# One-core diffusion backbone: the mask of local attention added in PSUM, softmax weights scaled on VectorE, and a reciprocal root taken as a power on GpSimd

## The reference

```python
def window_attention(q, k, v, kc, vc, sink):      # 8 heads of 64; one key head for 4 query heads
    valid = (abs(kj - T - qi) <= WINDOW) & (kpos >= 0) & (kpos < L)      # WINDOW = T = 128
    s_loc = where(valid, einsum(q, k) * scale, NEG)                      # scale = 1/8
    s_ctx = einsum(q, kc) * scale
    p = softmax(concatenate([s_loc, s_ctx, s_sink], -1))
    return einsum(p_loc, v) + einsum(p_ctx, vc)

def retention_out(o, g):                          # 8 heads of 64
    o = o * rsqrt(mean(o * o, -1) + EPS)
    return o * silu(g)
```

## Time and profile before

| | |
|---|---|
| median of 3 runs | 2737.83 us (2731.96 to 2738.38) |
| the profiled execution's own time | 2735.59 us |
| its span, first to last instruction | 2733.9 us |
| PE / DVE / ACT / POOL busy | 92% / 44% / 32% / 4% |
| mean granted TensorE clock | 0.950 of full speed |
| from the first score to the first product of the output projection | 914.36 to 1098.70 us |

### The profile page before, as it was taken

The page is one execution under the profiler, slowest core; times in us unless marked ns, Lnnn a source line. Parts: engine busy times, 40 slices in busy tenths (PEclk is TensorE's granted clock), DMA queues, the critical chain, the costliest instruction groups (busy, mean ns, idle before and its releaser), DMA issues.

```text
span 2733.9 us, 32899 instructions
## 1 busy us (share of the span) xinstructions
PE 2504.0 (92%) x12514; PEld 1971.3 (72%) x12514; DVE 1209.1 (44%) x1765; ACT 876.5 (32%) x1283; POOL 111.7 (4%) x186
## 2 busy tenths in 40 slices
PE   5899999999899887899999989999989828899997
PEld 2477788899778434778877778778878527788886
DVE  4523233565553676543222353323355385533334
ACT  1422222444431456343222242222244302422222
POOL 1011000000000110000011000100000000000000
PEclk9999999999999899889999989999979969799999
DMA  7566322455312000132356312552212113132322
GB/s 289 196 219 226 128 96 75 151 176 183 130 62 83 31 1 1 62 108 85 100 200 224 130 58 93 193 181 94 91 55 93 70 46 107 49 102 81 108 77 77
DMA packets 91167, 309.53 MB, mean 113 GB/s; under 512 B 10960, under 2 KB 11632, under 8 KB 89776
## 3 DMA queue, kind: packets, MB, share of 16 engines
q1 hardware_dynamic: 67824, 221.75, 24.2%
q0 software_dynamic: 21936, 84.88, 8.7%
q10 hardware_dynamic: 1296, 1.38, 0.1%
HBM read 299.58 MB, written 8.39 MB: 113 GB/s over the span
## 4 chain that ended last, share of the span: by engine, by line
PE 81%; DVE 8%; ACT 4%; DMA 2%; issue 2%; POOLq 0%; POOL 0%; DVEq 0%; ACTq 0%
PE psum L451 24%; PE psum L452 23%; PE psum L453 23%; PE psum L582 2%; DMA mod_raw<-in_w_mod 2%; PE psum L460 2%; PE psum L873 1%; DVE spectrum L359 1%; DVE term L352 1%; PE psum L740 1%; PE psum L604 1%; DVE w_lo L1297 1%; PE psum L862 1%; DVE stats L1767 1%; ACT w_hi L893 0%
## 5 line engine op out<-in xcount | busy, mean ns | idle before, releaser
L451 PE MATMUL psum<-h_hi,w_hi 128*128 128x512 f32 (+1 forms) x2256 | 860.4, 381 | 28.4 <-DVE h_lo L1480 13.7
L452 PE MATMUL psum<-h_lo,w_hi 128*128 128x512 f32 (+1 forms) x2256 | 848.4, 376 | 0.0
L453 PE MATMUL psum<-h_hi,w_lo 128*128 128x512 f32 (+1 forms) x2256 | 847.5, 376 | 0.0
L451 PEld LDWEIGHTS psum<-h_hi,w_hi 128*128 128x128 f32 x2256 | 429.3, 190 | 128.1 <-issue 35.1
L1297 DVE TENSOR_TENSOR w_lo<-raw,w_hi 128x1024 fp32r<-128x1024 f32 (+2 forms) x442 | 470.6, 1100 | 65.3 <-ACT w_hi L893 61.4
L893 ACT ACTIVATE w_hi<-raw 128x1024 fp32r<-128x1024 f32 (+2 forms) x442 | 405.8, 951 | 251.2 <-PE psum L453 243.7
L453 PEld LDWEIGHTS psum<-h_hi,w_lo 128*128 128x128 f32 x2256 | 429.1, 190 | 77.2
L452 PEld LDWEIGHTS psum<-h_lo,w_hi 128*128 128x128 f32 x2256 | 429.8, 191 | 74.0 <-issue 1.0
L451 PE MATMUL psum<-act_hi,w_hi 128*128 128x512 f32 (+1 forms) x880 | 331.5, 377 | 7.5 <-DVE w_lo L1297 5.5
L453 PE MATMUL psum<-act_hi,w_lo 128*128 128x512 f32 (+1 forms) x880 | 329.2, 374 | 0.0
L452 PE MATMUL psum<-act_lo,w_hi 128*128 128x512 f32 (+1 forms) x880 | 329.1, 374 | 0.0
(11 more groups left out here) (229 smaller groups left out, 1812.5 us busy)
## 6 DMA issues: line engine op xcount, KB each, us to landing
raw<-in_gate_up SPq DMA_DIRECT2D x220, 512.0 KB, 4.2
mod_raw<-in_w_mod POOLq DMA_DIRECT2D x144, 512.0 KB, 5.6
raw<-in_down_a SPq DMA_DIRECT2D x80, 384.0 KB, 3.5
raw<-in_down_b SPq DMA_DIRECT2D x80, 320.0 KB, 3.0
raw<-in_hy_in SPq DMA_DIRECT2D x24, 512.0 KB, 3.5
raw<-in_mix_in SPq DMA_DIRECT2D x22, 512.0 KB, 3.5
filt_dram<-made SPq DMA_DIRECT2D x6, 1024.0 KB, 3.8
filt<-filt_dram POOLq DMA_DIRECT2D x2, 3072.0 KB, 10.9
```

The source lines that it names most:

```text
L451: pe.matmul(out, w_hi[:, slot, c:c + P], hi, start=start, stop=False)
L452: pe.matmul(out, w_hi[:, slot, c:c + P], lo, start=False, stop=False)
L453: return pe.matmul(out, w_lo[:, slot, c:c + P], hi, start=False, stop=stop)
```

## The change

1. **Mask in PSUM.** `score` adds the mask to the own-key scores by one or two more matmuls (identity x mask tile, 128 columns each) in the same accumulation. The own keys now end where the context keys begin, so that the whole row is one stretch of PSUM (`score_row`). The masked score is scaled afterwards.
2. **Softmax order.** `take` is now only a maximum over PSUM and a small operation for the exponent's bias; `exps` reads PSUM and scales there. The division by the row sum moves from ACT to DVE, behind `take` of the next unit; ACT's order becomes `copy_out(s-1)`, `exps(s)`.
3. **Reciprocal root.** `root` on ACT becomes a scale and add (Identity); the four DVE reciprocals go; GpSimd raises the 128x512 tile to the power -0.5 in one instruction for each pair of heads.

```diff
-                    pe.matmul(psum[:, a, 0:(hi - lo) * P], q, k[:, lo * P:hi * P], start=True, stop=True)
+                    own = psum[:, a, SEQ - (hi - lo) * P:SEQ]
+                    pe.matmul(own, q, k[:, lo * P:hi * P], start=True, stop=False)
+                    if lo < n:
+                        pe.matmul(own[:, 0:P], ident[:, :], mask[:, 0:P], start=False, stop=hi == n + 1)
+                    if hi > n + 1:
+                        pe.matmul(own[:, (hi - lo - 1) * P:(hi - lo) * P], ident[:, :], mask[:, 2 * P:3 * P], start=False, stop=True)
...
                     act.wait_ge(scores_read, u + 1)
-                    act.activation(probs[:, i, 0:w], probs[:, i, 0:w], ACT.Exp, bias=stats[:, i, 1:2],
+                    if u >= 2:
+                        act.wait_ge(probs_turned, u - 1)
+                    act.activation(probs[:, i, 0:w], score_row(u), ACT.Exp, bias=stats[:, i, 1:2], scale=QK_SCALE,
                                    accum_out=stats[:, i, 2:3])
...
-                def normalize(u):
-                    w, i = window(u)[4], u % 2
-                    act.wait_ge(rsum_ready, u + 1)
-                    act.activation(probs[:, i, 0:w], probs[:, i, 0:w], ACT.Copy, scale=stats[:, i, 5:6]).then_inc(probs_ready, 1)
...
-                    act.activation(full[:, 1, :], psum[:, 7, :], ACT.Sqrt, bias=eps[:, 0:1],
+                    act.activation(full[:, 1, :], psum[:, 7, :], ACT.Identity, bias=eps[:, 0:1],
...
                     if 1 <= s <= UNITS:
-                        normalize(s - 1)
+                        copy_out(s - 1)
                     if s < UNITS:
                         exps(s)
-                    if 1 <= s <= UNITS:
-                        copy_out(s - 1)
...
-                    dve.scalar_tensor_tensor(probs[:, i, 0:own], psum[:, 2 * i, 0:own], QK_SCALE, mask[:, m:m + own], ALU.mult, ALU.add)
-                    seq(dve.tensor_scalar(probs[:, i, own:w], psum[:, 2 * i + 1, 0:CTX], QK_SCALE, None, ALU.mult))
-                    seq(dve.tensor_reduce(stats[:, i, 0:1], probs[:, i, 0:w], AX.X, ALU.max))
+                    seq(dve.tensor_reduce(stats[:, i, 0:1], score_row(u), AX.X, ALU.max))
...
-                    dve.reciprocal(stats[:, i, 5:6], stats[:, i, 4:5]).then_inc(rsum_ready, 1)
+                    seq(dve.reciprocal(stats[:, i, 5:6], stats[:, i, 4:5]))
+                    dve.tensor_scalar(probs[:, i, 0:w], probs[:, i, 0:w], stats[:, i, 5:6], None, ALU.mult).then_inc(probs_ready, 1)
...
-                    dve.reciprocal(full[:, 0, part], full[:, 1, part]).then_inc(dve_step, 1)
...
+            pool.memset(power[:, :], -0.5).then_inc(power_set, 1)
...
+            def invert(t):
+
+                pool.wait_ge(orms_ready, t + 1)
+                pool.tensor_tensor(full[:, 0, :], full[:, 1, :], power[:, 0:1].to_broadcast([P, SEQ]),
+                                   ALU.pow).then_inc(inv_ready, 1)
```

More of the change, by code:

```diff
@@ L208, in build @@
         stats = sb("stats", [P, 2, 8])
+        neg_sink = sb("neg_sink", [P, HEADS])
+        power = sb("power", [P, 1])
         filt_dram = nc.dram_tensor("filt_dram", (2, P, 3, 4, 512), F32).ap()
@@ L330, in build, with score_row @@
         osq_ready, osum_ready, orms_ready, oval_ready = map(sem, ("osq_ready", "osum_ready", "orms_ready", "oval_ready"))
+        def score_row(u):
+            i, w = u % 2, window(u)[4]
+            both = psum[:, 2 * i:2 * i + 2, :].rearrange("p b c -> p (b c)")
+            return both[:, SEQ + CTX - w:SEQ + CTX]
         def products(eng, step_sem, step, c, i, part, t0, t1, done, before):
@@ L731, in attention_retention @@
                 pe.wait_ge(result_read, at["p"] + BANKS)
+                pe.wait_ge(side_loaded, 32)
                 def score(u):
@@ L1759, in take @@
                 def take(u):
-                    h, n, lo, hi, w = window(u)
-                    own, m, i = w - CTX, (lo - n + 1) * P, u % 2
+                    h, i = window(u)[0], u % 2
                     dve.wait_ge(scores_ready, u + 1)
-                    if u >= 2:
-                        dve.wait_ge(probs_turned, u - 1)
-                    dve.scalar_tensor_tensor(probs[:, i, 0:own], psum[:, 2 * i, 0:own], QK_SCALE, mask[:, m:m + own], ALU.mult, ALU.add)
-                    seq(dve.tensor_scalar(probs[:, i, own:w], psum[:, 2 * i + 1, 0:CTX], QK_SCALE, None, ALU.mult))
-                    seq(dve.tensor_reduce(stats[:, i, 0:1], probs[:, i, 0:w], AX.X, ALU.max))
-                    dve.tensor_scalar(stats[:, i, 1:2], stats[:, i, 0:1], sink[:, h:h + 1], -1.0, ALU.max,
-                                      ALU.mult).then_inc(scores_read, 1)
+                    seq(dve.tensor_reduce(stats[:, i, 0:1], score_row(u), AX.X, ALU.max))
+                    dve.tensor_scalar(stats[:, i, 1:2], stats[:, i, 0:1], -QK_SCALE, neg_sink[:, h:h + 1], ALU.mult,
+                                      ALU.min).then_inc(scores_read, 1)
                 def normalize(u):
@@ L1805, in weigh @@
                         corner_of(2 * t + 3)
-                def invert(t, part):
-                    dve.wait_ge(orms_ready, t + 1)
-                    part = slice(part * P, part * P + P)
-                    dve.reciprocal(full[:, 0, part], full[:, 1, part]).then_inc(dve_step, 1)
-                    at["step"] += 1
                 def finish(t):
-                    dve.wait_ge(dve_step, at["step"])
+                    dve.wait_ge(inv_ready, t + 1)
                     seq(dve.tensor_tensor(prod[:, 0, :], prod[:, 0, :], full[:, 0, :], ALU.mult))
@@ L1825, in attention_retention @@
                 dve.wait_ge(gate_ready, 2)
+                seq(dve.tensor_scalar(neg_sink[:, :], sink[:, :], -1.0, None, ALU.mult))
                 corner_of(0)
@@ L1830, in attention_retention @@
                         att_out((s - 10) // 8)
+                    if s < UNITS:
+                        take(s)
                     if 1 <= s <= UNITS:
                         normalize(s - 1)
-                    if s < UNITS:
-                        take(s)
                     if s - INVERTED - 3 in PAIR_END:
@@ L1839, in attention_retention @@
                             weigh(i)
-                    for part in range(4):
-                        if s - 2 - part in PAIR_END:
-                            invert(PAIR_END.index(s - 2 - part), part)
                     if s - 2 - INVERTED in PAIR_END:
@@ L1960, in _ @@
                     ins.then_inc(table_ready, 1)
+                if t:
+                    invert(t - 1)
+            invert(HEADS // 2 - 1)
             pool.wait_ge(x_ready, 24)
```

3 lines of the change are left out of this document (2 added, 1 removed).

## The result

The changed kernel takes **2986.42 us** (median of 4 runs, 2984.69 to 2990.32) against 2735.37 (2731.96 to 2738.38) for the kernel before beside it: ratio 1.092, 95% interval 1.0901 to 1.094. It is 251 us slower. The prediction had the direction right, but at 2791 (2744 to 2862) not the size.

What follows compares the result with a forecast made beforehand. The prediction took the mixer's stage to be bound by a chain between engines. Order +4, power's hold +42 and half clock +8 gave +54 on 2735.6, 2789.6; with 2.2 for the median, 2791 us, range 2744 to 2862.

Steps and rivals of the forecast that it cites:

- the price of the power: GpSimd's power for each pair: 15 us long, 4.6 of it free, so 4 x (15 - 4.6) = +42.
- the rival with "30 us or more": GpSimd's power far longer, 30 us or more: over +116, 2855 and up; chance 0.10.
- The mechanism: A running GpSimd power holds VectorE's sum and scaling, now on the chain before the transposes, until it ends: +42.
- a power that doesn't hold VectorE: Rival: the power is hidden, within the free 4.6 us or not holding VectorE: +4, 2742; chance 0.20.
- a remark: By its dependencies the power holds up little: `finish` comes 22 us after `root`, the last wanted some 16 us after.
- The half clock term (8): TensorE at half clock behind four holes of 10 us left by the powers, about 2 each: +8.
- The order of the softmax: Mask products and the new softmax order in the mixer's stage, without the power: +4, bounds -4 to +12.
- The clear steps: Score-to-score times without stalls: long units 5.6 even, 6.4 to 6.6 odd; short 4.8 and 5.7 to 5.8.
- The decay adds on the chain: GpSimd's decay adds meet VectorE's sum and scaling on the chain, once for each of three pairs: +4.5.
- The old stalls of 24: Stalls before the change from decay tables, function table switches, held VectorE adds and half clock: 24 us, taken as gone.
- +1.5 for half clock at the start: TensorE's mask products at half clock at the start of the stage: +1.5.
- The rival "TensorE's rest is not in series": Mixer steps return to 5.16 and 4.46 without stalls, power hidden: about 2715; chance 0.05 for faster by over 0.3%.

Runs made afterwards that it cites:

- the multiply kernel: The changed kernel with GpSimd's power replaced by a plain multiply of the same tile, so the root is left out: 2745.39 us, ratio 1.0052.
- the kernel with short adds: The changed kernel with a multiply for the power, and GpSimd's decay adds of the last three pairs on 32 of 512 columns: 2739.25 us, ratio 1.002.

## Why the prediction was wrong, and where it was right

**The step that failed is the price of the power.** "A power is a logarithm and an exponential at least, so I take 15 us, with 7 and 30 as the ends": it is 81.93 us, 5.5 times the estimate and 2.7 times its upper end. The estimate scaled VectorE's reciprocal (5.9 times a plain operation) to GpSimd; against GpSimd's plain add of 1.26 the power is 65 times as long. No row of before was near it, the upper end of 30 had nothing behind it, and the rival with "30 us or more" had a chance of 0.10.

**The mechanism failed too.** "A power of 15 us would hold it for what is left of 15 us": it holds nothing. The prediction had named this sign itself (sums that stay at 0.16 beside a running power), and what came was a mixture of two of its rivals: a power that doesn't hold VectorE, and one far longer than 30 us. The row behind it was read rightly (a VectorE add held to the end of a GpSimd add; short and long plain adds both bear it out), but it was carried over from one operation to another. The Trainium skill ("SBUF — State Buffer", section "Who interferes with whom") gives the ports that VectorE and GpSimd share to one instruction as a lock for its whole length, and names VectorE's instructions with two SBUF inputs, as the sum is, among those that need them. These runs agree for plain adds (sum 1.02, scaling 1.27) and disagree for the power (0.15 and 0.55 beside it), and the measurement decides. Why the power doesn't hold them wasn't tried.

**What did set the price** stands in the prediction as a remark: `finish` comes 22 us after `root`, and the last one is wanted 16 us after. With a power of 81.9 us these slacks give 3 x 60 + 66 = 246, and 2735.6 + 4 + 246 + 2.2 = 2988, 1.4 above the measured median. That it comes so near is luck in part: the order was +14 and not +4, and the waits 242 and not 246. Measured waits are 57.1, 57.9, 58.4 and 68.9, slacks 24.8, 24.1, 23.5 and 13.0. The hold would have made the power's price 4 x (81.9 - 4.6) = 309. So with the right size and the wait of `finish` in place of the hold, the sum would have come out within a few us. The half clock term (8) isn't to be seen in the difference: the kernel with power is 241.0 above the one with a multiply, its waits 241.5. Half clock does stand behind the holes (the transposes at 1056.97, behind 58.71 idle, take 1.33), but in the multiply kernel they take 1.33 at that place too, behind the hole that the decay adds leave, and the step that follows takes 7.01 in both.

**The order of the softmax** was +4 (-4 to +12) and measured +14 without the root's cost (+18 with it), just outside its bounds. The clear steps were right: 5.34 to 5.51 and 6.39 to 6.61 for long ones (5.6; 6.4 to 6.6), 4.8 to 5.0 and 5.64 for short ones (4.8; 5.7 to 5.8); eight of them from step 3 on make 44.7 in the kernel with short adds (44.4). Mis-sized are its stalls. The decay adds on the chain were put at 4.5 and gave 6.1. "The old stalls of 24 are not in it" was only partly so: from the third to the last score the multiply kernel takes 173.9 where 161 and the 4.5 were expected, and 168.6 remain with short adds. Two single steps make some 3 us of the rest: the third score's own takes 6.99, its products at half clock, where other even long steps take 5.34 to 5.51 (the prediction's +1.5 for half clock at the start belongs there), and step 29 takes 8.01 where other odd long steps take 6.39 to 6.61 (9.68 in the kernel with short adds). What remains is spread and wasn't taken apart. Steps 28 and 29 have no retention scores. TensorE's rows there, in the multiply kernel:

```profile
1084.99 0.76 PE L761 MATMUL psum<-ident,probs 128*128 128x128 f32 x5 [2.02 <-DVE probs L1781]
...
1090.36 0.77 PE L761 MATMUL psum<-ident,probs 128*128 128x128 f32 x5 [2.02 <-DVE probs L1781]
1091.05 1.86 PE L774 MATMUL psum<-probs_t,av 128*64 128x128 f32 x20
1092.69 1.06 PE L795 MATMUL psum<-sumsq,rv 128*64 128x512 f32 x1
```

With nothing to do between score and transposes, TensorE is idle for 2.02 twice, and then `pv` takes 1.86 instead of 1.31, at a mean granted clock of 0.61 from 1091 to 1094; the sum had no term for such a step. The tail (+1.2) was right, from the last score to the projection 10.45 against 9.27; the gain of 1.4 at the start didn't come (the first two steps 12.1 against 11.9). Two slips in the prediction's sums change nothing: 2789.6 + 2.2 is 2791.8, and "4 x 25 + 12" is 112 and not over 116.

**Where the order's own parts go.** The prediction took its cost as one chain, and the runs split it: mask in PSUM -12.6, VectorE's scaling 0, copy ahead of exps -5, `take` ahead of `normalize` +32, the root's loads and reciprocals gone -4. They add up to +10 where +14 was measured, as near as runs of three sets can be added; the -4 is small too, since the runs of its two kernels overlap (2741.95 to 2747.64 and 2745.44 to 2754.05). One exchange of two calls on VectorE eats the gains of all others and more. The rival "TensorE's rest is not in series" set its mark at "when the transposes start by T + 2.5". With them at T + 2.78 an even step is 4.49, so the mark was about right, but its mechanism wasn't: in that kernel TensorE's products follow one another in series without an idle time, and the step is short because nothing in the series waits for VectorE. The change was one exchange of two calls away from it.

## What to carry to other kernels

When an operation is moved to an engine on which no row shows it, price it by its slack instead of by a guess at its length: say how long it may be before somebody waits (here 13 to 25 us), and give no upper end to what it may cost beyond that; a run with a single short instruction of that kind on that engine would have settled it. In an in-order queue, put the work whose consumer is idle now (sum and scaling of the last row) ahead of the work for the next round; here that is worth 32 to 36 us out of 2730, more than the mask (12.6) or the root's reciprocals (4) gained. A contention seen between two operations is a fact about these two and is to be measured again for a third.

## What the runs showed of the hardware

- GpSimd's power of f32 takes 20.74, 41.13 and 81.93 us for 128, 256 and 512 columns: 160 to 162 ns a column, nearly in proportion. A multiply of 128x512 with the same broadcast operand took 1.05 us, so the operation alone is 78 times as long.
- During the power VectorE's adds of one column (0.15) and its scaling of 128x640 (0.55) kept their usual times. Beside plain GpSimd adds a sum took 1.02 and such a scaling 1.32. No VectorE instruction that reads two wide tiles from SBUF ran beside a power, so for those nothing is shown.
- TensorE's clock fell not only behind long holes: in the multiply kernel two idle stretches of 2.02, 5.4 us apart, in steps without retention scores, stood before a `pv` of 1.86 instead of 1.31 and retention values of 1.06 instead of 0.59, at a mean granted clock of 0.61 (1.2 GHz is 0.5, 2.4 GHz is 1).
